# Gate and up of a feed-forward by seven products of quarters (the Winograd form of Strassen's scheme) in a two-block fp32 kernel

## The chip, the cores and the metric

The kernel runs on one core of a Trainium2 chip. The metric is the device time of one execution in microseconds (us); lower is better. All arithmetic is fp32.

## The reference

Two transformer blocks work on x of 256 tokens by 1024. The change concerns the last piece of the second block:

```
h = modulate(rms_norm(x, g_ffn), sh_f, sc_f)
x = x + gt_f * ((silu(h @ w_gate) * (h @ w_up)) @ w_down)
```

w_gate and w_up are 1024 by 2816, w_down is 2816 by 1024. sh_f, sc_f and gt_f are slices of silu(c) @ w_ada + b_ada; only gt_f, the last of them, is made while the feed-forward runs.

## The kernel before, in words

The program is one list of instructions for each engine, written out by hand and tied by semaphores. Every engine works its list in order, so a wait holds everything behind it on that engine.

**Weights.** Weights of 2 MB (a "tile": 8 chunks of 128 rows by 512 columns, or 4 by 1024) stream through a ring of three slots (`wring`, `W_SLOTS`), in the order of `TILES` (`tile_list`, L98), issued by SP at L455. The load of tile n waits until tile n-3 is no longer needed. For the feed-forward the order is gate0, up0, gate1, up1, ada10, gate2, up2, ada11, gate3, ... up5, down0 to down5. gate5, up5 and down5 are half tiles. ada10 and ada11 are two of the twelve parts of w_ada; DVE multiplies each by the row c and sums it, in four chunks of 128x1024 (`ada_sums`, L1553). When ada11 is done, POOL writes the row gt_f out and reads it back to all partitions (`gate_row`, L1433 and L1436); DVE needs it when down is finished.

**Products.** hT2 holds h turned: 8 chunks of 128 features by 256 tokens. Gate and up are made turned too: a 128x128 block of weights is the stationary operand, and chunks of hT2 stream past it. `by_cols` (L543) streams all 256 tokens at once, 8 chunks for each of the 4 column blocks of a tile. `by_block` (L613) streams one block of 128 tokens; gate0 and up0 are made so, since the second block of tokens is turned late (`turn_fed`). An fp32 product stands in the trace as two records of a weight load and two of a matmul.

**Elementwise work.** For each half tile ACT takes the tanh of half the gate sum from PSUM (L1402), DVE multiplies (1 + tanh) by the gate sum (L2178) and that by the up sum (L2181), which gives gT; the factor 0.5 comes in at the end. PSUM banks rotate by `PLAN` and `bank_list`. Down (L1079) takes gT as stationary operand and streams 512 columns of w_down at a time into four sums; DVE scales them by gt_f and adds them to x (L2149, L2150), and SP stores x.

**Just before the feed-forward**, PE makes the last product of w_out (L1041), DVE adds it to x (L2149, L2150), ACT takes the norm, DVE scales (L1495), PE turns the block (L520), and DVE modulates it into hT2 (L1504, L1508).

## Time and profile before

| | |
|---|---|
| median of 3 runs | 1334.63 us (1334.06 to 1335.1) |
| the profiled execution, its own time | 1332.32 us |
| its span, first to last instruction | 1330.5 us |
| PE busy | 1211.0 us (91%) |
| DVE busy | 791.2 us (59%) |
| ACT busy | 231.9 us (17%) |
| moved by DMA | 401 MB, 302 GB/s |
| mean granted clock of PE | 0.973 of 2.4 GHz |

The span is what the trace shows; the profiled execution took 1.8 us more than it, and the median of the runs is 2.3 us above the profiled execution. In the rows below L12 is a line of the kernel before; PE is TensorE's matmuls, PEld its weight loads, which run beside them; DVE, ACT, POOL and SP are the vector, scalar, GpSimd and sync engines. In square brackets or behind the last bar stands the idle time ahead of an instruction and what ended it.

### The profile page before, as it was taken

The numbers are of one execution on the slowest core, as the hardware profiler recorded it, in microseconds if no ns is written. First come the engines' busy times: TensorE is split into PE (matmuls) and PEld (weight loads), VectorE is DVE, ScalarE is ACT, GpSimd is POOL, SyncE is SP. The second block draws the span as 40 slices with busy tenths as digits, with TensorE's granted clock in tenths as the row PEclk, the third lists the DMA queues.
The fourth block names the chain that finished last, engine by engine and source line by source line (L and its number), as shares of the span: only waits on it lengthen the run. The fifth ranks groups of instructions, "written<-read, shape, count | busy, mean of one in ns | idle before, by whom it ended". The sixth has DMA issues, their size and how long they took to land.

```text
span 1330.5 us, 12510 instructions
## 1 busy us (share of the span) xinstructions
PE 1211.0 (91%) x4454; PEld 730.4 (55%) x4454; DVE 791.2 (59%) x1886; ACT 231.9 (17%) x593; POOL 321.6 (24%) x276
## 2 busy tenths in 40 slices
PE   8999999988988887777988887688999899999998
PEld 7657996654554443333333333333466559888743
DVE  4667864589686887686877865655557932220001
ACT  2132210221111111113111112113102511000000
POOL 0100000334544544344445355541000000000000
PEclk9999999999999999799999899989999999999999
DMA  8531658799999999999999999998658534574540
GB/s 312 184 133 64 253 200 321 291 373 406 418 421 420 421 423 415 416 420 410 418 421 422 397 405 422 421 420 339 231 190 252 206 127 156 191 223 143 190 158 32
DMA packets 93789, 401.27 MB, mean 302 GB/s; under 512 B 6496, under 2 KB 9952, under 8 KB 60832
## 3 DMA queue, kind: packets, MB, share of 16 engines
q0 software_dynamic: 37440, 270.30, 49.3%
q1 hardware_dynamic: 56288, 130.18, 27.5%
q8 instruction: 36, 0.59, 0.2%
q14 instruction: 25, 0.20, 0.0%
HBM read 399.39 MB, written 1.06 MB: 301 GB/s over the span
## 4 chain that ended last, share of the span: by engine, by line
PE 60%; DMA 21%; DVE 14%; issue 2%; ACT 2%; POOL 1%; DVEq 0%; SPq 0%
DMA big<-in_peer_uv,idx_t 20%; PE ps L543 18%; PE ps L818 12%; PE ps L531 8%; DVE big L1941 6%; PE ps L1079 6%; PE ps L613 3%; PE ps L691 2%; PE ps L722 2%; PE ps L1041 2%; PE ps L749 2%; PE ps L591 1%; POOL big L1454 1%; DMA wring<-in_w_in 1%; ACT rows L1247 1%
## 5 line engine op out<-in xcount | busy, mean ns | idle before, releaser
L818 PE MATMUL ps<-big,rows 128*128 128x512 f32 x1024 | 482.4, 627 | 107.3 <-ACT rows L1247 107.2
L818 PEld LDWEIGHTS ps<-big,rows 128*128 128x128 f32 x1024 | 199.9, 200 | 371.8 <-issue 371.8
L1454 POOL DMA_INDIRECT big<-in_peer_uv,idx_t x256 | 310.3, 1212 | 377.3 <-PE ps L818 323.0
L1941 DVE CUSTOM_DVE_ANT_0 big<-big 128x1024 f32<-128x1024 f32 x256 | 307.9, 1226 | 139.6 <-DMA big<-in_peer_uv,idx_t 136.7
L543 PE MATMUL ps<-big,wring 128*128 128x256 f32 x1088 | 236.8, 379 | 0.0
L543 PEld LDWEIGHTS ps<-big,wring 128*128 128x128 f32 x1088 | 206.0, 190 | 28.0 <-issue 0.5
L531 PE MATMUL ps<-wring,big 128*128 128x512 f32 (+1 forms) x304 | 126.0, 571 | 0.0
L1241 ACT ACTIVATE small<-small 128x4 f32<-128x4 f32 (+2 forms) x68 | 13.9, 205 | 502.3 <-DVE small L1946 502.3
L531 PEld LDWEIGHTS ps<-wring,big 128*128 128x128 f32 x304 | 57.0, 190 | 62.8 <-issue 61.0
L1247 ACT ACTIVATE rows<-const,small 128x128 f32<-128x128 f32 x256 | 82.2, 390 | 21.1 <-DVE small L1950 21.1
L1079 PE MATMUL ps<-wring,big 128*128 128x512 f32 x176 | 75.7, 592 | 0.0
L2149 DVE SCALAR_TENSOR_TENSOR big<-ps,big 128x512 f32<-128x512 f32 x8 | 5.5, 692 | 91.3 <-PE ps L1079 70.6
L1432 POOL TENSOR_TENSOR small<-small,lane 128x8 f32<-128x8 f32 x2 | 1.2, 624 | 232.2 <-DVE small L1553 232.2
L2181 DVE TENSOR_TENSOR big<-big,ps 128x512 f32<-128x512 f32 x11 | 7.6, 688 | 82.1 <-PE ps L543 74.8
L1079 PEld LDWEIGHTS ps<-wring,big 128*128 128x128 f32 x176 | 33.4, 190 | 41.7 <-issue 41.6
L1553 DVE CUSTOM_DVE_ANT_0 wring<-wring,c_row 128x1024 f32<-128x1024 f32 x40 | 47.2, 1220 | 6.4 <-DMA wring<-in_w_ada 5.0
L749 PEld LDWEIGHTS ps<-big,wring 128*128 128x128 f32 x384 | 46.0, 192 | 9.1 <-issue 9.1
L749 PE MATMUL ps<-big,wring 128*128 128x128 f32 x384 | 46.3, 275 | 0.0
L1127 ACT ACTIVATE big<-ps 128x512 f32<-128x512 f32 (+1 forms) x57 | 31.0, 582 | 73.9 <-PE ps L531 23.8
L613 PE MATMUL ps<-big,wring 128*128 128x128 f32 x320 | 36.3, 275 | 1.0 <-DVE big L1504 1.0
L613 PEld LDWEIGHTS ps<-big,wring 128*128 128x128 f32 x320 | 36.0, 192 | 1.7 <-DVE big L1504 1.2
L1418 POOL DMA_DIRECT2D big<-in_norm_ffn x1 | 0.7, 692 | 137.3 <-DVE big L1736 137.3
(287 smaller groups left out, 988.2 us busy)
## 6 DMA issues: line engine op xcount, KB each, us to landing
wring<-in_w_in SPq DMA_DIRECT2D x16, 2048.0 KB, 8.5
wring<-in_w_ada SPq DMA_DIRECT2D x10, 2048.0 KB, 7.9
wring<-in_w_gate SPq DMA_DIRECT2D x5, 2048.0 KB, 7.7
wring<-in_w_up SPq DMA_DIRECT2D x5, 2048.0 KB, 9.0
wring<-in_w_down SPq DMA_DIRECT2D x5, 2048.0 KB, 7.6
wring<-in_peer_wq SPq DMA_DIRECT2D x4, 2048.0 KB, 20.8
wring<-in_w_out SPq DMA_DIRECT2D x3, 2048.0 KB, 8.4
big<-in_peer_uv,idx_t POOLq DMA_INDIRECT x256, 13.0
```

Source lines behind the costliest of these rows:

```text
L531: last = nc.tensor.matmul(o[:, 0:w], lhs[:, c, b * P:(b + 1) * P], wt[:, c, c0:c0 + w], start=(c == 0), stop=(c == k - 1))
L543: last = nc.tensor.matmul(o[:, c2 * S:(c2 + 1) * S], wt[:, c, n0:n0 + P], src[:, c, :], start=(c == 0), stop=(c == KD - 1))
L613: last = nc.tensor.matmul(o[:, c2 * S + b * P:c2 * S + (b + 1) * P], wt[:, c, n0:n0 + P], src[:, c, b * P:(b + 1) * P], start=(c == 0), st ...
L691: last = nc.tensor.matmul(o[:, c2 * S:(c2 + 1) * S], wt[:, c, n0:n0 + P], lhs[:, c, :], start=(c == 0), stop=(c == 3))
L749: last = nc.tensor.matmul(o[:, n * P:(n + 1) * P], wt[:, c, n * P:(n + 1) * P], h2T[b][:, c, :], start=(c == 0), stop=(c == KD - 1))
L818: last = nc.tensor.matmul(banks[h], diag[:, k % DIAGS, :], v_part[:, ring_at(k), h * 512:(h + 1) * 512], start=False, stop=(k % SLOTS == S ...
L1079: last = nc.tensor.matmul(o, gT[:, f, b * P:(b + 1) * P], wt[:, c, h * 512:(h + 1) * 512], start=(f == 0), stop=(f == FC - 1))
L1127: nc.scalar.activation(dst, bank(name, n) if src is None else src, ACT.Copy).then_inc(emptied(*name), 1)
L1247: nc.scalar.activation(diag[:, k % DIAGS, :], ident, ACT.Copy, scale=w_now[:, at_w:at_w + 1])\
L1454: pool.indirect_dma_start(pair_ring[:, ring_at(k), :], None, a["peer_uv"], bass.IndirectOffsetOnAxis(idx_t[:, k:k + 1], 0))\
L1553: last = nc.vector.tensor_tensor_reduce(w[:, c, :], w[:, c, :], c_row[:, :], 1.0, 0.0, ALU.mult, ALU.add, to[:, c:c + 1])
L1941: nc.vector.tensor_tensor_reduce(u_part[:, ring_at(k), :], u_part[:, ring_at(k), :], h_t[:, b, :], 1.0, 0.0, ALU.mult, ALU.add, a_dot[:, i ...
```

## The change

Each of gate0, gate1, up1, ... gate5, up5 (eleven tiles, numbered j = 0 to 10; up0 stays as eight plain products of each column block and token block) is cut into quarters: two halves f of its columns by two halves k of the 1024 features. hT2 is cut into two halves k by two blocks of tokens b. Seven products of quarters (P1 to P7, `step`) take the place of eight. Each product is 4 chunks for each of 2 column blocks of 128, all with 128 tokens streamed (half tiles: 1 column block).

- DVE makes four sums of weight quarters for each tile (`weight_sums`), each of 4x256 elements a partition, the fourth in place in the ring slot; and four sums of hT2 once (`h_sum`).
- P1, P6, P7 and P4 pile up in one pair of banks, P5 and P3 in another, P2 has its own. After P1, P5, P6, P7 and P4, ACT copies the running sum of 128x256 to SBUF (`part_out`); DVE adds three pairs (`part_added`).
- The gate sum lies in SBUF (ff_g). tanh, its product with (1 + tanh) and the product with up are now one instruction each of 128x1024 for a tile.
- The tiles ada10 and ada11 leave the ring: both go to one buffer of their own, ada10 behind gate1 and ada11 behind gate3. For ada11 SP waits until DVE has summed all of ada10. The ring has up1 right before gate2 and up2 right before gate3. One chunk of 128x1024 of ada10 or ada11 is summed with each of the tiles j = 1 to 8.
- Down has the same products in other banks. It waits for gT tile by tile.

The core of the diff (new buffers, views of them, semaphores and the last loop of DVE, which has the same work as before, are left out):

```diff
@@ -48,7 +48,28 @@
-FF_ADA = {1: 10, 2: 11}
+FF_PRODUCTS = [("gate", 0)] + [(n, i) for i in range(1, 6) for n in ("gate", "up")]
+FF_ADA = {j: (10 + (j - 1) // 4, (j - 1) % 4) for j in range(1, 9)}
+HOME_COUNT = {4: 1, 5: 2, 10: 3, 11: 4}
+FF_ORDER = [("P1", "P2", "P5", "P6", "P3", "P7", "P4")] + [("P1", "P5", "P6", "P3", "P7", "P2", "P4")] * 10
+def pairs_of(i):
+    return min(4, FC - 4 * i) // 2
+def ff_steps(j, product):
+    return 7 * j + FF_ORDER[j].index(product) + 1
+def ff_banks(j):
+    return 2 * (j % 2), 4, 6 + j % 2
@@ -117,8 +138,6 @@
         t += [(f"gate{i}", KD, w, "w_gate", 0, 512 * i), (f"up{i}", KD, w, "w_up", 0, 512 * i)]
-        if i in FF_ADA:
-            t += [ada[FF_ADA[i]]]
     t += [(f"down{i}", min(4, FC - 4 * i), D, "w_down", 512 * i, 0) for i in range(6)]
...
+                    elif before != "up0" and before[:-1] in ("gate", "up"):
+                        sp.wait_ge(step_done, 7 * (FF_PRODUCTS.index((before[:-1], int(before[-1]))) + 1))
...
+                if name in ("gate1", "gate3"):
+                    i = 10 if name == "gate1" else 11
+                    if i == 11:
+                        sp.wait_ge(ada_made, ADA_ORDER.index(10) + 1)
+                    p0 = 512 * ADA_PARTS[i]
+                    sp.dma_start(ada_home2.rearrange("p (c n) -> p c n", c=4),
+                                 a["w_ada"][p0:p0 + 512, :].rearrange("(c p) n -> p c n", p=P)).then_inc(home_landed, 16)
...
@@ -1054,32 +1124,113 @@
-            for h in range(2):
-                reserved("gate0", h)
-            by_block("gate0", 0, hT2)
...
+                sums, w = ff_sums(j), pairs_of(FF_PRODUCTS[j][1])
+                x_bank, z_bank, y_bank = ff_banks(j)
...
+                if product == "P1":
+                    n = TILE_NO["%s%d" % FF_PRODUCTS[j]]
+                    pe.wait_ge(tile_landed[n % W_SLOTS], 16 * (n // W_SLOTS + 1))
+                    if j >= 2:
+                        pe.wait_ge(part_copied, 5 * (j - 1))
+                    else:
+                        bank_free(x_bank)
+                        bank_free(x_bank + 1)
+                    lhs, rhs, o, start = ff_quarter(j, 0, 0), hT2[:, k0, tok[0]], x_bank, True
+                elif product == "P2":
+                    if j >= 2:
+                        pe.wait_ge(part_added, 3 * (j - 1))
+                    else:
+                        bank_free(y_bank)
+                    lhs, rhs, o, start = ff_quarter(j, 0, 1), hT2[:, k1, tok[0]], y_bank, True
+                elif product == "P5":
+                    pe.wait_ge(w_summed, 4 * j + 1)
+                    if j:
+                        pe.wait_ge(part_added, 3 * (j - 1) + 1)
+                    else:
+                        bank_free(z_bank)
+                        bank_free(z_bank + 1)
+                        pe.wait_ge(h_summed, 1)
+                    lhs, rhs, o, start = sums[:, 0], h_sum[:, 0], z_bank, True
+                elif product == "P6":
+                    pe.wait_ge(w_summed, 4 * j + 2)
+                    if j == 0:
+                        pe.wait_ge(h_summed, 2)
+                    pe.wait_ge(part_copied, 5 * j + 1)
+                    lhs, rhs, o, start = sums[:, 1], h_sum[:, 1], x_bank, False
+                elif product == "P3":
+                    pe.wait_ge(w_summed, 4 * j + 3)
+                    pe.wait_ge(part_copied, 5 * j + 2)
+                    lhs, rhs, o, start = sums[:, 2], hT2[:, k1, tok[1]], z_bank, False
+                elif product == "P7":
+                    pe.wait_ge(w_summed, 4 * j + 4)
+                    if j == 0:
+                        pe.wait_ge(h_summed, 3)
+                    pe.wait_ge(part_copied, 5 * j + 3)
+                    lhs, rhs, o, start = ff_quarter(j, 1, 0), h_sum[:, 2], x_bank, False
+                else:
+                    if j == 0:
+                        pe.wait_ge(h_summed, 4)
+                    pe.wait_ge(part_copied, 5 * j + 4)
+                    lhs, rhs, o, start = ff_quarter(j, 1, 1), h_sum[:, 3], x_bank, False
+                for n in range(w):
+                    to = ps[:, o, n * P:(n + 1) * P] if product == "P2" else ps[:, o + n, 0:P]
+                    for c in range(4):
+                        last = nc.tensor.matmul(to, lhs[:, c, n * P:(n + 1) * P], rhs[:, c, :], start=(start and c == 0),
+                                                stop=(c == 3), skip_group_check=True)
+                last.then_inc(step_done, 1)
+            def up_first(b, quarters):
+                wt = tile("up0", KD, 512)
+                for n in quarters:
+                    h, c2 = n // 2, n % 2
+                    o = ps[:, BANK[("up0", h)], :]
+                    for c in range(KD):
+                        last = nc.tensor.matmul(o[:, c2 * S + b * P:c2 * S + (b + 1) * P], wt[:, c, n * P:(n + 1) * P],
+                                                hT2[:, c, b * P:(b + 1) * P], start=(c == 0), stop=(c == KD - 1))
+                    if b == NB - 1 and c2:
+                        begin("up0", h)
+                        last.then_inc(product_done, 1)
+            step(0, "P1")
+            step(0, "P2")
+            reserved("up0", 0)
+            up_first(0, (0,))
             turn_fed(1)
-            for h in range(2):
-                reserved("up0", h)
-            by_block("up0", 0, hT2)
-            wait_turned("n5T", [1])
-            by_block("gate0", 1, hT2)
-            by_block("up0", 1, hT2)
-            for i in range(1, 6):
-                by_cols(f"gate{i}", TILES[TILE_NO[f"gate{i}"]][2], hT2)
-                by_cols(f"up{i}", TILES[TILE_NO[f"up{i}"]][2], hT2)
-            outs = [begin("down", b, h) for b in range(NB) for h in range(2)]
+            up_first(0, (1,))
+            reserved("up0", 1)
+            up_first(0, (2, 3))
+            for product in ("P5", "P6", "P3", "P7"):
+                step(0, product)
+            up_first(1, (0, 1))
+            step(0, "P4")
+            up_first(1, (2, 3))
+            for j in range(1, len(FF_PRODUCTS)):
+                for product in FF_ORDER[j]:
+                    step(j, product)
             for i in range(6):
-                pe.wait_ge(ff_ready, min(2 * i + 2, FC // 2))
-                for n, o in enumerate(outs):
+                pe.wait_ge(ff_ready, i + 1)
+                if i == 0:
+                    pe.wait_ge(part_copied, 5 * (end - 2))
+                    pe.wait_ge(part_added, 3 * (end - 1))
...
@@ -1393,14 +1544,32 @@
                 act.wait_ge(x_whole, 5 + b)
                 rms(4, b)
             exp_and_tanh()
-            for i in range(6):
-                for h in range(2 if i < 5 else 1):
-                    n = 2 * i + h
-                    wait_product(act, f"gate{i}", h)
-                    if n >= 1:
-                        act.wait_ge(ff_ready, n)
-                    nc.scalar.activation(ff_e, bank((f"gate{i}", h)), ACT.Tanh, scale=0.5).then_inc(ff_exp, 1)
+            def part_out(j, product, n, to):
+                act.wait_ge(step_done, ff_steps(j, product))
+                nc.scalar.activation(to, sums_in(j, n), ACT.Copy).then_inc(part_copied, 1)
+            def gate_tanh(j):
+                i = FF_PRODUCTS[j][1]
+                act.wait_ge(part_added, 3 * j + 3)
+                act.wait_ge(part_copied, 5 * j + 5)
+                w = 512 * pairs_of(i)
+                nc.scalar.activation(ff_e[:, 0:w], ff_g[:, 0:w], ACT.Tanh, scale=0.5).then_inc(ff_exp, 1)
+            for j, (kind, i) in enumerate(FF_PRODUCTS):
+                if j >= 2:
+                    act.wait_ge(part_added, 3 * (j - 1))
+                part_out(j, "P1", 0, part_at(j, 0))
+                part_out(j, "P5", 1, part_at(j, 1))
+                if j >= 2 and kind == "up":
+                    gate_tanh(j - 1)
+                part_out(j, "P6", 0, part_at(j, 2))
+                part_out(j, "P7", 0, part_at(j, 3))
+                if kind == "gate" and i:
+                    act.wait_ge(ff_ready, i)
+                part_out(j, "P4", 0, ff_out(j, 1, 0))
+                if j == 0:
+                    gate_tanh(0)
...
@@ -2161,37 +2330,108 @@
+            def weight_sums(j, which):
+                sums, q = ff_sums(j), [[ff_quarter(j, f, k) for k in range(2)] for f in range(2)]
+                n = TILE_NO["%s%d" % FF_PRODUCTS[j]]
+                if which[0] == 0:
+                    dve.wait_ge(tile_landed[n % W_SLOTS], 16 * (n // W_SLOTS + 1))
+                    if j >= 2:
+                        dve.wait_ge(step_done, 7 * (j - 1))
+                for m in which:
+                    if m == 0:
+                        tt(sums[:, 0], q[1][0], q[1][1], ALU.add).then_inc(w_summed, 1)
+                    elif m == 1:
+                        dve.wait_ge(w_summed, 4 * j + 1)
+                        tt(sums[:, 1], sums[:, 0], q[0][0], ALU.subtract).then_inc(w_summed, 1)
+                    elif m == 2:
+                        dve.wait_ge(w_summed, 4 * j + 2)
+                        tt(sums[:, 2], q[0][1], sums[:, 1], ALU.subtract).then_inc(w_summed, 1)
+                    else:
+                        tt(q[1][0], q[0][0], q[1][0], ALU.subtract).then_inc(w_summed, 1)
             mixed_added(0, 0)
             mixed_added(1, 0)
             scale(4, 0)
             mixed_added(0, 1)
             dve.wait_ge(modc_ready, 2)
             turned("n5T", 0, hT2, modc[:, 3 * KD:4 * KD], modc[:, 2 * KD:3 * KD])
+            weight_sums(0, (0, 1, 2))
             mixed_added(1, 1)
+            weight_sums(0, (3,))
             scale(4, 1)
             turned("n5T", 1, hT2, modc[:, 3 * KD:4 * KD], modc[:, 2 * KD:3 * KD])
-            for i in range(6):
-                for h in range(2 if i < 5 else 1):
-                    n = 2 * i + h
-                    dve.wait_ge(ff_exp, n + 1)
-                    link(stt(ff_e, ff_e, 1.0, bank((f"gate{i}", h)), ALU.add, ALU.mult))
-                    dve.sem_inc(emptied(f"gate{i}", h), 1)
-                    wait_product(dve, f"up{i}", h)
-                    tt(gT[:, 2 * n:2 * n + 2, :].rearrange("p c t -> p (c t)"), ff_e, bank((f"up{i}", h)), ALU.mult)\
-                        .then_inc(ff_ready, 1)
-                    dve.wait_ge(ff_ready, n + 1)
-                    dve.sem_inc(emptied(f"up{i}", h), 1)
-                if i in FF_ADA:
-                    ada_sums(FF_ADA[i], range(4))
+            for h in range(2):
+                wait_moved(dve, "n5T", 1, h)
...
+            tt(h_sum[:, 0], fed[0][1], fed[0][0], ALU.subtract).then_inc(h_summed, 1)
+            dve.wait_ge(h_summed, 1)
+            tt(h_sum[:, 1], fed[1][1], h_sum[:, 0], ALU.subtract).then_inc(h_summed, 1)
+            tt(h_sum[:, 2], fed[1][1], fed[0][1], ALU.subtract).then_inc(h_summed, 1)
+            dve.wait_ge(h_summed, 2)
+            tt(h_sum[:, 3], fed[1][0], h_sum[:, 1], ALU.subtract).then_inc(h_summed, 1)
+            def gated(j):
+                dve.wait_ge(ff_exp, i + 1)
+                stt(ff_g[:, 0:w], ff_e[:, 0:w], 1.0, ff_g[:, 0:w], ALU.add, ALU.mult).then_inc(ff_gated, 1)
+            def fed_out(j):
+                dve.wait_ge(part_copied, 5 * j + 5)
+                dve.wait_ge(part_added, 3 * j + 3)
+                dve.wait_ge(ff_gated, i + 1)
+                to = gT[:, 4 * i:4 * i + 2 * pairs_of(i), :].rearrange("p c t -> p (c t)")
+                tt(to, to, ff_g[:, 0:w], ALU.mult).then_inc(ff_ready, 1)
+            for j, (kind, i) in enumerate(FF_PRODUCTS):
+                ahead = j + 1 < len(FF_PRODUCTS)
+                if ahead:
+                    weight_sums(j + 1, (0, 1))
+                if j == 1:
+                    gated(0)
+                    dve.wait_ge(ff_gated, 1)
+                    for h in range(2):
...
+                        last = tt(gT[:, 2 * h:2 * h + 2, :].rearrange("p c t -> p (c t)"), ff_g[:, h * 512:(h + 1) * 512],
+                                  bank(("up0", h)), ALU.mult)
+                        last.then_inc(emptied("up0", h), 1)
...
+                    dve.sem_inc(ff_ready, 1)
+                elif kind == "up":
+                    gated(j - 1)
+                elif j > 1:
+                    fed_out(j - 1)
+                if kind == "gate" and i:
+                    dve.wait_ge(ff_ready, i)
+                dve.wait_ge(step_done, ff_steps(j, "P3"))
+                dve.wait_ge(part_copied, 5 * j + 3)
+                tt(ff_out(j, 0, 1), part_at(j, 2), sums_in(j, 1), ALU.add).then_inc(part_added, 1)
+                if ahead:
+                    weight_sums(j + 1, (2, 3))
+                if j in FF_ADA:
+                    n, c = FF_ADA[j]
+                    ada_sums(n, [c])
+                dve.wait_ge(part_copied, 5 * j + 4)
+                tt(ff_out(j, 1, 1), part_at(j, 3), part_at(j, 1), ALU.add).then_inc(part_added, 1)
+                dve.wait_ge(step_done, ff_steps(j, "P2"))
+                tt(ff_out(j, 0, 0), part_at(j, 0), sums_in(j, 2), ALU.add).then_inc(part_added, 1)
+            fed_out(len(FF_PRODUCTS) - 1)
...
```

## Rows read from the trace of the kernel before

**Rows 1.** The page: span, PE busy, granted clock in 40 slices.
```profile
span 1330.5 us, 12510 instructions
...
PE 1211.0 (91%) x4454; PEld 730.4 (55%) x4454; DVE 791.2 (59%) x1886; ACT 231.9 (17%) x593; POOL 321.6 (24%) x276
...
PEclk9999999999999999799999899989999999999999
```

**Rows 2.** Chain that ended last: start us, us, what, records.
```profile
1097.31 7.14 PE ps L613 x64
...
1105.33 21.44 PE ps L613 x192
1126.77 124.32 PE ps L543 x576
1251.09 75.55 PE ps L1079 x176
```

**Rows 3.** Stretches: us, busy by engine (records), PEclk, DMA share, GB/s.
```profile
1105.33:1126.77 21.44, 21.44 (x193) 21.44 (x193) 4.35 (x7) 1.19 (x2) 0.00 (x0) 1.00 0.28 99
1126.77:1251.09 124.32, 124.32 (x577) 109.44 (x577) 21.73 (x34) 5.37 (x9) 1.73 (x3) 1.00 0.56 190
324.00:330.00 6.00, 3.99 (x7) 1.69 (x7) 5.53 (x17) 1.96 (x6) 1.27 (x2) 0.79 1.01 416
330.00:336.00 6.00, 6.00 (x23) 3.29 (x22) 5.39 (x24) 1.63 (x6) 3.08 (x4) 0.93 1.04 409
```

**Rows 4.** Timeline of PE among the experts: start us, us, what, records.
```profile
326.12 8.80 PE L818 MATMUL ps<-big,rows 128*128 128x512 f32 x16 [2.01 <-ACT rows L1247]
...
335.65 1.95 PE L749 MATMUL ps<-big,wring 128*128 128x128 f32 x16
337.44 7.03 PE L818 MATMUL ps<-big,rows 128*128 128x512 f32 x16
```

**Rows 5.** Groups by line and shape, DVE: busy us, mean ns, idle.
```profile
L1553 DVE CUSTOM_DVE_ANT_0 wring<-wring,c_row 128x1024 f32<-128x1024 f32 x40 | 47.2, 1220 | 6.4 <-DMA wring<-in_w_ada 5.0 <-DVE big L2041 0.7 <-DVE big L2181 0.4
...
L2181 DVE TENSOR_TENSOR big<-big,ps 128x512 f32<-128x512 f32 x11 | 7.6, 688 | 82.1 <-PE ps L543 74.8 <-PE ps L613 7.3
...
L1666 DVE TENSOR_TENSOR big<-big 128x1024 f32<-128x1024 f32 x4 | 4.9, 1219 | 0.0
...
L2125 DVE TENSOR_TENSOR big<-ps,small 128x256 f32<-128x256 f32 x4 | 1.7, 425 | 0.1
```

**Rows 6.** The same view, ACT.
```profile
L1152 ACT ACTIVATE big<-big 128x1024 f32<-128x1024 f32 x2 | 2.1, 1057 | 6.5 <-DVE big L1565 6.5
...
L1127 ACT ACTIVATE big<-ps 128x256 f32<-128x256 f32 x4 | 1.6, 389 | 11.1 <-PE ps L782 10.2 <-PE ps L790 0.9
```

**Rows 7.** Waits, 1128 to 1250 us: total us, times, longest us.
```profile
DVE big L2181 <- PE ps L543: 69.2, 8, 12.5
```

**Rows 8.** DMA issues, 947.7 to 948.5 us: count, KB, us to landing.
```profile
wring<-in_w_in SPq DMA_DIRECT2D x1, 2048.0 KB, 8.4
big<-in_w_ada SPq DMA_DIRECT2D x1, 2048.0 KB, 13.1
```

**Rows 9.** DMA issues, 200 to 215 us.
```profile
wring<-in_w_out SPq DMA_DIRECT2D x1, 2048.0 KB, 10.0
big<-in_w_out SPq DMA_DIRECT2D x1, 2048.0 KB, 14.9
```

**Rows 10.** Timeline of POOL at the last modulation row.
```profile
1188.19 0.97 POOL L1433 DMA_DIRECT2D gate_out<-small  x1 [0.30 <-POOL small L1432]
```

**Rows 11.** DMA issue of gate4 at 1187.64 us.
```profile
wring<-in_w_gate SPq DMA_DIRECT2D x1, 2048.0 KB, 12.3
```

**Rows 12.** Timeline ahead of the feed-forward, DVE.
```profile
1092.99 0.69 DVE L1508 TENSOR_TENSOR big<-big,small 128x512 f32<-128x512 f32 x1
...
1097.35 0.69 DVE L2149 SCALAR_TENSOR_TENSOR big<-ps,big 128x512 f32<-128x512 f32 x1 [3.67 <-PE ps L1041]
...
1100.61 0.75 DVE L1495 TENSOR_SCALAR big<-x_t,rstd 128x1024 f32<-128x1024 f32 x1 [1.84 <-ACT rstd L1123]
```

More of the change, by code:

```diff
@@ L176, in product_list @@
     p += [("out2_0", 0), ("catT", 1), ("out2_1", 0), ("out2_0", 1)] + half("n5T", 0)
-    p += [("out2_1", 1)] + half("n5T", 1) + cols("gate0") + cols("up0")
-    for i in range(1, 6):
-        for n in (f"gate{i}", f"up{i}"):
-            p += cols(n, 2 if i < 5 else 1)
-    p += [("down", b, h) for b in range(NB) for h in range(2)]
+    p += [("out2_1", 1)] + half("n5T", 1) + cols("up0")
     return p
 PLAN = {name: n for n, name in enumerate(product_list())}
+LAST_BANKS = {("out2_0", 1): 6, ("n5T", 0, 0): 2, ("n5T", 0, 1): 3, ("out2_1", 1): 7, ("n5T", 1, 0): 4, ("n5T", 1, 1): 5,
+              ("up0", 0): 2, ("up0", 1): 3}
 def bank_list():
@@ L197, in bank_list @@
             bank[name] = 4
+        elif name in LAST_BANKS:
+            bank[name] = LAST_BANKS[name]
         elif name == ("n3T", 1, 0):
@@ L327, in two_blocks @@
         gT = at(big, 2048, FC * S).rearrange("p (c t) -> p c t", c=FC)
-        ff_e = at(big, 7680, 512)
+        ff_sum = [at(big, 8192 + 3072 * i, 3072) for i in range(2)]
+        h_sum = at(big, 14336, 2048).rearrange("p (n c t) -> p n c t", n=4, c=4)
+        parts = [at(big, 16384 + 1024 * i, 1024) for i in range(2)]
+        ff_g, ff_e = at(big, 18432, 1024), at(big, 19456, 1024)
+        ada_home2 = at(big, 22528, TILE)
         tmp2 = at(big, 28416, 1024)
@@ L1070, in _, with bank_free, step @@
-            outs = [begin("down", b, h) for b in range(NB) for h in range(2)]
+            def bank_free(n):
+                pe.wait_ge(bank_emptied[n], sum(v == n for v in BANK.values()))
+            def step(j, product):
+                sums, w = ff_sums(j), pairs_of(FF_PRODUCTS[j][1])
+                x_bank, z_bank, y_bank = ff_banks(j)
+                k, tok = (slice(4 * n, 4 * n + 4) for n in range(2)), [slice(b * P, (b + 1) * P) for b in range(NB)]
+                k0, k1 = k
+                if product == "P1":
[49 more added lines that the diff above has]
+                last.then_inc(step_done, 1)
@@ L1071, in _ @@
+            end = len(FF_PRODUCTS)
             for i in range(6):
-                k = TILES[TILE_NO[f"down{i}"]][1]
+                k = 2 * pairs_of(i)
                 wt = tile(f"down{i}", k, D)
-                pe.wait_ge(ff_ready, min(2 * i + 2, FC // 2))
-                for n, o in enumerate(outs):
+                pe.wait_ge(ff_ready, i + 1)
+                if i == 0:
+                    pe.wait_ge(part_copied, 5 * (end - 2))
+                    pe.wait_ge(part_added, 3 * (end - 1))
+                for n, o in enumerate(DOWN_BANKS):
@@ L2187, in _ @@
-            dve.wait_ge(mod_ready, 32)
-            for b in range(NB):
-                for h in range(2):
-                    wait_product(dve, "down", b, h)
-                    if b == 1:
-                        dve.wait_ge(x_ready, h + 1)
-                    gated_add(bank(("down", b, h)), mod[:, 1, :], b, slice(h * 512, (h + 1) * 512),
-                              tmp2[:, h * 512:(h + 1) * 512], 0.5).then_inc(x_ready, 1)
+            for h in range(2):
+                wait_moved(dve, "n5T", 1, h)
@@ new lines, in _ @@
+            fed = [[hT2[:, 4 * k:4 * k + 4, b * P:(b + 1) * P] for b in range(NB)] for k in range(2)]
+            tt(h_sum[:, 0], fed[0][1], fed[0][0], ALU.subtract).then_inc(h_summed, 1)
[4 more added lines that the diff above has]
+            tt(h_sum[:, 3], fed[1][0], h_sum[:, 1], ALU.subtract).then_inc(h_summed, 1)
@@ new lines, in _ @@
+            fed_out(len(FF_PRODUCTS) - 1)
+            dve.wait_ge(mod_ready, 32)
+            for n in range(2 * NB):
+                b, h = n // 2, n % 2
+                c = slice(h * 512, (h + 1) * 512)
+                t = tmp2[:, h * 512:(h + 1) * 512]
+                dve.wait_ge(last_done, n + 1)
+                if b == 1:
+                    dve.wait_ge(x_ready, h + 1)
+                link(stt(t, ps[:, DOWN_BANKS[n], :], 0.5, mod[:, 1, c], ALU.mult, ALU.mult))
+                tt(x[:, b, c], x[:, b, c], t, ALU.add).then_inc(x_ready, 1)
```

50 lines of the change are left out of this document (42 added, 8 removed).

## Prediction

> **What bounds the kernel now.** I read the page first, then the chain of waits, then the stretches. The page has PE busy for 91% of the span at nearly full clock [rows 1]. The chain from the end of the last w_out product on is PE alone: 7.14 + 21.44 us of 128-token pieces, 124.32 us of 256-token pieces, 75.55 us of down [rows 2]. In both gate and up stretches PE is busy for the whole time at a granted clock of 1.00 (the 2.4 GHz level), with DVE busy for a fifth or less [rows 3]. Others wait for PE there and PE for nobody: DVE alone 69.2 us in 8 waits [rows 7]. So here time is PE time, as long as what the change gives DVE, ACT and the loads stays beside it.
>
> **PE's work.** The pieces of 128 tokens (L613) are 64 + 192 records in 28.58 us, 111.6 ns each, so one product (two records) takes 223.3 ns. Those of 256 tokens (L543) are 576 records in 124.32 us, 215.8 ns each, 431.7 ns a product [rows 2]. Together 152.9 us. After the change all pieces have 128 tokens: gate0 56, up0 64, eight full tiles 8 x 56 = 448, two half tiles 2 x 28 = 56, in sum 624 products x 223.3 ns = 139.3 us. PE gains 13.6 us: an eighth of the work goes (17.9 us), the narrower pieces give 4.3 us back, since the weight loads fill the whole of such a stretch (PEld 21.44 of 21.44 us against 109.44 of 124.32 us [rows 3]).
>
> Does the rate hold with much going on beside it? Among the experts 16 records of the same shape take from 335.65 to 337.44, 111.9 ns each [rows 4], with DMA at 409 GB/s and DVE busy for 90% [rows 3]. I take 111.6.
>
> **DVE and ACT.** One full tile takes PE 56 x 0.2233 = 12.50 us, a product of quarters (8 pieces) 1.79 us. DVE's sum of two 128x1024 operands costs 1.22 us, 512 wide 0.69, 256 wide 0.43 (from PSUM; I take it for the SBUF pair too), a chunk of w_ada 1.22 [rows 5]. For each full tile DVE has four sums (4.9), one gating product (1.2), three additions (1.3), one chunk (1.2): 8.6 us of 12.5. ACT has five copies at 0.39 and every second tile a tanh of 1.06 [rows 6]: 2.5 us on average. A copy lies beside the next product, which uses other banks: 0.39 + about 0.1 of signals against 1.79. The closest chain in steady state: DVE's third addition of a gate tile, tanh, the copy of P6, P7. P7 starts 7.15 us into the up tile, so the tanh may start as late as 7.15 - 0.05 - 0.39 - 1.06 = 5.6 us into it; the addition is done 0.8 us ahead of the tile. All this I cost at nothing; the cover is the 3.9 us that DVE has free in each tile.
>
> **The start.** DVE's three sums for gate0 stand between the modulation of the first token block, done at 1092.99 + 0.69, and the last w_out addition, which began at 1097.35 [rows 12]: 3.66 us in a hole of 3.67. Allow 0.15 us. The fourth sum lies in the 1.84 us in which DVE waits for the norm [rows 12]. PE comes to the second turning after 24 pieces, at 1097.31 + 5.36 = 1102.67; the scaling is done by about 1101.5. The sums of hT2 (4 x 0.69) are started by 1106 and the first is ready at about 1106.7; P5 of gate0 needs it at 1108.9. Cost nothing. up1 can only be loaded when gate0's P4 is through, 24.1 us after 1097.31, and takes 8.4 us as a lone load [rows 8]. DVE stands at it until 32.6, and its P3 addition of gate1 comes at about 38; P5 of up1 needs that at 42.0. Cost nothing, with 4 us to spare.
>
> **The ring at up3.** Here I expect a stall. SP may issue ada11 only when DVE has summed the last chunk of ada10, in the tile up2, and up3 stands behind ada11 in SP's list. Count from the end of up2 on PE. P3 of up2 ends at -5.35; DVE then adds (0.43), makes two sums (2.44) and the chunk (1.22), and with signals SP issues ada11 at about -0.9, up3 0.4 later. Two loads issued together landed 8.4 and 13.1 us after issue [rows 8], elsewhere 10.0 and 14.9 [rows 9]: the second about 5 us behind the first. So up3 lands at about 12.6. DVE's very next item at 0 is the sums of up3, so it stands for 12.6 us with gate3's additions behind it. Then two sums (2.44), the gating of up2 (1.22) and gate3's first addition (0.43) with signals: 16.9. That addition frees the bank pair that P5 of up3 wants. PE ends gate3 at 12.5, waits about 0.2 for up3 itself, makes P1 until 14.5 and stands until 16.9: **2.4 us**. The rest of DVE's list (two sums, chunk, two additions) ends at 21.5, then tanh and the P6 copy end at 23.0, where P7 could have begun at 22.3: **0.7 us**. Together about 3.4 us. gate4, issued behind up3, lands 5 us after it, at 17.7, and DVE wants it at 21.4: nothing more.
> Bounds: no stall at all, if ada11 goes out early or up3 overtakes it; or up3 a full lone load (8.4 us) after ada11 in place of 5, 3.3 us more, so 6.7 us. I take 3.4, from the pairs of loads.
>
> **The rest.** Down begins when up5 ends; down0 is issued as up4 ends, 12.5 us before it is wanted. Beside the write of gt_f [rows 10] a load took 12.3 us [rows 11], and the same write now falls there: 0 to 0.5 us, I take 0. Down (75.55 us) and the last additions stay. Waits already met cost PE nothing in the alternation of rows 4. ACT copies and takes exp among the experts with no table load between them, so the copies bring none.
>
> **The sum.** -13.6 + 3.4 = -10.2 us; signals and the start 0.1. The profiled execution, 1332.3 us (span 1330.5 [rows 1]), would take 1322.2. The median of the runs is 2.3 us above it: 1324.5 us.
>
> **The rivals.**
> *No stall at up3*: the whole 13.6 us, 1321.0 us. For it: the loads leave the DMA half idle (share 0.56 [rows 3]). Against it: the order of SP's and DVE's lists.
> *A longer stall at up3*: the bound of 6.7 us, and perhaps the clock. In the stretch from 324 us, with a wait of 2.01 us, the clock stood at 0.79 [rows 3] and 16 wide records took 8.80 us against 7.03 [rows 4]: 1.8 us more. That is 1334.6 - 13.6 + 6.7 + 1.8 = 1329.5 us.
> *PE shows its waits*: 77 products start behind waits that PE did not have. At 0.1 us each, 7.7 us more: 1332 us, no change. Against it stand rows 4, where such waits cost nothing. From 0.13 us each there is no gain left.
> *DVE becomes the bound, and the kernel slower*: the place is the sums and gating products, five a tile. At a price s DVE's tile is 5s + 3 us with signals, against 12.5: it binds from s = 1.9. Before that the stall at up3 grows with s, so at 1.9 the gain is used up. If the four-chunk views, one of them written into the ring slot beside PE's reads, doubled the price to 2.44, the tile would be 15.2 us: 8 x 2.7 = 21.6 us, and a longer stall at the start and at up3 of about 7, less the 13.6 gained and some overlap, gives about 1350 us. Against it: 1.22 us in every row of that size, chunks written in a ring slot included [rows 5].
> *Narrow pieces cost more than half of wide ones*: the change makes 992 more records of 128 tokens. At 0.6 of a wide record in place of 0.52 (129.5 ns for 111.6) they take 17.8 us more, 1342 us. Against it: the rate of rows 2 and 4. The Trainium skill (TensorE: Matmul & The Clock Gate, Back-to-back issue gap) gives 81 ns for 128 columns and 131 ns for 512 in a stream of bf16 loads and matmuls; an estimate on a straight line between them is 98 ns for 256, so that half the width costs 0.83 of the whole, which here would be 67 us over the forecast, about 1391 us. The trace disagrees for fp32: 111.6 against 215.8 ns, 0.52.
>
> **How the numbers follow.** Forecast with a stall of 2 to 5 us: 0.63. No stall: 0.08. Longer stall: 0.15. Waits shown: 0.07. DVE bound: 0.06. Narrow pieces: 0.01. The range 1320.5 to 1330.5 takes the first three. A measurement of this kernel can tell 0.2%, 2.7 us. Faster: the first three and a fourth of the waits' case, 0.88; same 0.05; slower 0.07.
>
> **What would show it.** Some 1248 records of 128 tokens at 111.6 ns, no 256-token records in gate and up. DVE's sums at 1.22 us, ACT's copies at 0.39. One DMA wait of DVE of about 12 us for the tile of w_up, behind it one PE wait of some 2.4 us ended by a DVE addition and one under 1 us ended by an ACT copy; up3 landing near 13 us after issue. Down starting about 10 us earlier. The forecast is wrong if PE idles ahead of most products, if the sums take over 1.5 us, or if a second tile's load is waited for on PE.

## The result, and the profile after

The changed kernel takes 1345.0 us (median of 4 runs, 1344.52 to 1347.55) where the kernel before takes 1334.82: a ratio of 1.0083, 95% interval 1.007 to 1.0095 (all ratios here are worked out from the single runs, not from the two medians, which give 1.0076). It is slower by 10 us; the forecast was 10 us faster, 1324.5 us in a range of 1320.5 to 1330.5. All ratios are of fast runs: one run of the kernel before, of the 13 beside e5 to e8, took 4420 us in the slow state and is left out of them. The span of its profiled execution is 1342.7 us, 12.2 more than before [rows 1]. In what follows the changed kernel's lines are: L1184 the matmuls of the seven products, L1195 those of up0, L1230 down, L1111 w_out, L590 the turning of the norm; on DVE L2343, L2346, L2349 and L2351 are the four sums of a tile, L2379 and L2389 the gating products, L2400 the products with up0, L2414 the addition that frees the banks of P5 and P3, L2421 and L2423 the other two, L1722 a chunk of w_ada; L1550 on ACT copies a partial sum.

The chain of waits of the changed kernel, from the last w_out product on (start us, us, what; compare [rows 2]):

```profile
1093.99 6.87 PE ps L1111 x16
1100.86 3.57 PE ps L1184 x32
...
1123.17 1.80 PE ps L1184 x16
1124.97 0.02 issue
1124.99 7.72 DMA wring<-in_w_up
...
1136.39 1.30 DVE big L2400 x2
1137.68 0.14 issue
1137.82 46.98 PE ps L1184 x400
...
1189.09 13.11 DMA wring<-in_w_up
...
1205.88 0.43 DVE big L2414
1206.31 0.14 issue
1206.44 37.61 PE ps L1184 x320
1244.06 0.02 issue
1244.07 17.21 DMA wring<-in_w_down
1261.29 0.04 issue
1261.33 77.51 PE ps L1230 x176
```

Before, this chain was PE alone. Now it runs three times through a load. The same three places in the timeline of PE (in square brackets PE's idle time and what ended it), with one ahead of them:

```profile
1086.01 7.11 PE L1111 MATMUL ps<-wring,big 128*128 128x512 f32 x16 [1.60 <-DVE x_t L2319]
...
1137.82 3.75 PE L1184 MATMUL ps<-big,wring 128*128 128x128 f32 x16 [9.29 <-DVE big L2400]
...
1206.44 7.22 PE L1184 MATMUL ps<-big 128*128 128x128 f32 x48 [2.01 <-DVE big L2414]
...
1220.65 5.52 PE L1184 MATMUL ps<-big 128*128 128x128 f32 x48
...
1261.33 0.99 PE L1230 MATMUL ps<-wring,big 128*128 128x512 f32 x1 [4.78 <-DMA wring<-in_w_down]
```

Stretches of the changed kernel, in the columns of rows 3:

```profile
1137.80:1141.40 3.60, 3.58 (x17) 3.60 (x18) 0.00 (x0) 0.00 (x0) 0.00 (x0) 0.50 0.00 0
...
1141.40:1204.27 62.87, 62.87 (x561) 62.84 (x560) 30.95 (x39) 11.11 (x26) 0.00 (x0) 0.99 0.43 154
1204.27:1213.50 9.23, 7.22 (x50) 7.09 (x49) 9.16 (x12) 2.49 (x5) 0.00 (x0) 0.82 0.88 327
```

**Where the 12.2 us came from.** Gate and up, from the end of w_out to the start of down, took 1097.31 to 1251.09 before, 153.8 us, and 1100.86 to 1261.33 now, 160.5 us. The matmuls are what was counted: the stretch from 1141.40 has 561 records in 62.87 us, 112 ns each, and 139.3 us + 0.9 us of turning make 140.2. The other 20.3 us are waits and the clock behind them: 9.3 us at gate1 and 1.8 us since its first 16 records take 3.54 us (1137.82 to 1141.36) and not 1.79; 2.0 us at up3 and 1.7 us in the 48 records behind it (7.22 us against 5.52 in a later tile); 4.8 us at down0; 0.7 us in smaller parts. Down takes 77.5 us in place of 75.6, again with a lowered clock. The 3.5 us by which the stage starts later are 1.6 us of the wait at 1086, 0.6 us of clock (the first and the third of the four w_out products take 7.21 and 7.11 us, not 6.87), and 1.4 us by which the first w_out product started later, at 1069.89 against 1068.53 us. These 1.4 us say nothing of the change: in two executions of one and the same kernel further down (e4 and e12) that start is at 1070.98 and at 1068.87. In sum 6.7 + 2.0 + 3.5 = 12.2.

### The profile page after: what moved, and what is told of

Read it like the earlier page. It is cut to its first block, busy times and chain, and to the rows that moved or that the text cites. A ratio compares the mean times of both kernels' runs of the same rounds, so it can differ in the third digit from the quotient of the medians.

```text
span 1342.7 us, 13525 instructions
## 1 busy us (share of the span) xinstructions
PE 1206.8 (90%) x4870; PEld 737.7 (55%) x4870; DVE 849.9 (63%) x1958; ACT 250.8 (19%) x643; POOL 319.9 (24%) x276
## 4 chain that ended last, share of the span: by engine, by line
PE 53%; DMA 25%; DVE 17%; issue 2%; ACT 2%; POOL 1%; SPq 0%; DVEq 0%; ACTq 0%
DMA big<-in_peer_uv,idx_t 20%; PE ps L888 9%; PE ps L613 8%; PE ps L601 8%; PE ps L1184 7%; DVE big L2110 7%; PE ps L1230 6%; PE ps L1111 2%; PE ps L761 2%; PE ps L792 2%; PE ps L819 2%; DMA wring<-in_w_up 2%; DMA wring<-in_w_in 1%; DMA wring<-in_w_down 1%; PE ps L661 1%
## 5 line engine op out<-in xcount | busy, mean ns | idle before, releaser
L613 PE MATMUL ps<-big,wring 128*128 128x256 f32 x512 | 112.3, 379 | 0.0
L613 PEld LDWEIGHTS ps<-big,wring 128*128 128x128 f32 x512 | 96.6, 190 | 13.2 <-issue 0.5
L1184 PE MATMUL ps<-big,wring 128*128 128x128 f32 x640 | 75.6, 279 | 9.3 <-DVE big L2400 9.3
L1230 PE MATMUL ps<-wring,big 128*128 128x512 f32 x176 | 77.5, 603 | 4.8 <-DMA wring<-in_w_down 4.8
L1184 PEld LDWEIGHTS ps<-big,wring 128*128 128x128 f32 x640 | 74.3, 195 | 9.9 <-DVE big L2400 9.4
L1230 PEld LDWEIGHTS ps<-wring,big 128*128 128x128 f32 x176 | 33.9, 193 | 47.7 <-issue 42.7
L1184 PE MATMUL ps<-big 128*128 128x128 f32 x480 | 57.5, 281 | 2.0 <-DVE big L2414 2.0
L1184 PEld LDWEIGHTS ps<-big 128*128 128x128 f32 x480 | 56.6, 198 | 2.2 <-issue 2.2
L2433 DVE SCALAR_TENSOR_TENSOR big<-ps,big 128x512 f32<-128x512 f32 x4 | 2.8, 691 | 77.0 <-PE ps L1230 77.0
L819 PEld LDWEIGHTS ps<-big,wring 128*128 128x128 f32 x384 | 46.0, 192 | 9.1 <-issue 9.1
L819 PE MATMUL ps<-big,wring 128*128 128x128 f32 x384 | 46.3, 275 | 0.0
L1550 ACT ACTIVATE big<-ps 128x256 f32<-128x256 f32 (+1 forms) x55 | 19.9, 365 | 125.6 <-PE ps L1184 119.1
```

Of the source, the lines that this page charges most:

```text
L613: last = nc.tensor.matmul(o[:, c2 * S:(c2 + 1) * S], wt[:, c, n0:n0 + P], src[:, c, :], start=(c == 0), stop=(c == KD - 1))
L819: last = nc.tensor.matmul(o[:, n * P:(n + 1) * P], wt[:, c, n * P:(n + 1) * P], h2T[b][:, c, :], start=(c == 0), stop=(c == KD - 1))
L1184: last = nc.tensor.matmul(to, lhs[:, c, n * P:(n + 1) * P], rhs[:, c, :], start=(start and c == 0), stop=(c == 3), skip_group_check=True)
L1230: last = nc.tensor.matmul(ps[:, o, :], gT[:, f, b * P:(b + 1) * P], wt[:, c, h * 512:(h + 1) * 512], start=(f == 0), stop=(f == FC - 1))
```

## The experiments

The kernels e1 to e4 were run together, then e5 to e8, then e9 to e12. Each batch had the kernel before beside it, with medians of 1333.86, 1334.86 and 1334.59 us. Ratios are to that, with 95% intervals. The changed kernel itself was not run in these batches, so a difference to its 1345.0 us is good to about 1 us; the traces, between two marks of the same execution, tell more.

**The wait at gate1.** In DVE's loop, gate0's gating and the products with up0 ahead of the sums of up1:

```diff
-                if ahead:
+                if ahead and j != 1:
                     weight_sums(j + 1, (0, 1))
                 if j == 1:
...
                     dve.sem_inc(ff_ready, 1)
+                    weight_sums(2, (0, 1))
```

> The changed kernel with one reordering in DVE's list: at gate1 the gating of gate0 and its product with up0 stand ahead of the weight sums of up1, not behind them. Theory (the first product of gate1 wants the banks that up0 was summed in, and DVE empties them only after it has waited for the load of up1): PE's wait of 9.3 us at the start of gate1 falls to about 1.5 us, the 1.8 us of lowered clock behind it go too, 9 to 10 us less than the changed kernel: about 1335.5 us. Rival (PE stands there for the load of up1 itself or for the sums made from it): the wait stays near 9 us and the time near 1345 us.

Measured: 1336.19 us, 1.0019 (1.0006 to 1.0031), against 1345.0 for the changed kernel. The timeline of PE:

```profile
1130.66 2.02 PE L1184 MATMUL ps<-big,wring 128*128 128x128 f32 x16 [0.87 <-DVE big L2400]
```

That is 8.8 us less, 9 to 10 were expected. The wait fell from 9.29 to 0.87 us and the 16 records from 3.75 to 2.02. The load of up1 takes as long as it did; PE did not need it. P1 of gate1 writes banks 2 and 3 (`ff_banks(1)`), and the change gives these to up0 too (`LAST_BANKS`). DVE's products with up0 empty them, and stood behind the sums of up1, which wait for its load. Here DVE still waits for up1's load until 1134.26 us, 3.6 us after PE has begun gate1; so the rival, that PE needs the load itself or the sums made from it, is out.

**The wait at down0.** POOL's last step:

```diff
             pool.wait_ge(ada_made, ADA_ORDER.index(11) + 1)
+            pool.wait_ge(down_used, 2)
             gate_row(1)
```

> The changed kernel with POOL's write and reading back of the last modulation row held until two tiles of down are used up; DVE needs the row only at the end. Theory (the 4 KB write in pieces of 4 bytes, issued 1.9 us ahead of down0, slows down0's load from about 8 to 17.2 us): down0 lands 8 to 9 us after issue, PE's 4.8 us wait for it goes and the 2 us of lowered clock in down as well, 1338 to 1340 us. Rival (the loads of down are slow at this place by themselves): down0 still takes over 14 us and the time stays near 1345 us.

Measured: 1338.52 us, 1.0038 (1.0027 to 1.005). 6 to 7 us less than the changed kernel's, as expected. PE has no wait at down0, and the stage reads, in its chain:

```profile
1207.36 50.10 PE ps L1184 x432
1257.46 75.55 PE ps L1230 x176
```

Down is back at 75.55 us. The landing of down0, first here, then in the changed kernel (DMA issues at 1244.98 and 1244.07 us):

```profile
wring<-in_w_down SPq DMA_DIRECT2D x1, 2048.0 KB, 9.2
```

```profile
wring<-in_w_down SPq DMA_DIRECT2D x1, 2048.0 KB, 17.2
```

POOL's write in the changed kernel:

```profile
1242.18 0.97 POOL L1602 DMA_DIRECT2D gate_out<-small  x1 [0.30 <-POOL small L1601]
```

It is issued 1.9 us ahead of down0, and its signal lets POOL go on at 1252.43 us. From 1244.07 to 1252.40 us the DMA engines move 35 GB/s at a busy share of 0.46; from there to 1261.30 us 330 GB/s at 0.89. With the row late, 1244.00 to 1252.40 us has 252 GB/s. So the load hardly moved until the write was done, and then took about what a lone load takes.

To see which half of POOL's step does it, only the reading back was held:

```diff
                 pool.wait_ge(gates_out, 16 * (j + 1))
+                if j == 1:
+                    pool.wait_ge(down_used, 2)
                 pool.dma_start(mod[:, j, :], gate_out[j].partition_broadcast(P)).then_inc(mod_ready, 16)
```

> The changed kernel in which POOL writes the last modulation row out at once, as there, but reads it back to all partitions only after two tiles of down. Theory (the write in pieces of 4 bytes alone slows down0's load): down0 still lands 15 to 18 us after issue, PE still waits 4 to 5 us for it, time near 1345 us. Rival (the reading back of 512 KB is what down0 shares the queues with): down0 lands in 9 to 13 us, no wait, 1338 to 1340 us.

Measured: 1345.95 us, 1.0078 (1.0057 to 1.0099); down0 landed after 16.0 us, PE waited 3.6 us for it. So the write of 4 KB alone makes most of the delay: 16.0 us against the 8.0 to 9.3 us of the seven traces in which the write comes later (e2, e4, e8 to e12). The four traces of kernels with both halves of the step there have 17.2, 17.4, 17.7 and 18.3 us, so reading back seems to add 1 to 2 us; that rests on a single trace of e6.

**The stall at up3, the one that was forecast.** ada11 moved behind up3 in SP's list:

```diff
-                if name in ("gate1", "gate3"):
+                if name in ("gate1", "up3"):
```

> The changed kernel with the load of ada11 moved in SP's list from behind gate3 to behind up3, so that up3 waits for nothing but its slot. Theory of the prediction (up3 lands late because it stands behind a wait for DVE's last sum of ada10 and then behind ada11 in the queue, DVE stands for it, and PE stands for DVE's addition that frees its banks): DVE's 12.9 us wait goes, PE's 2.0 us wait with it and the 1.7 us of lowered clock behind it, about 1341 us. Rival (the stall at up3 is made up later, since DVE has slack): about 1345 us, with PE's time spent at another wait.

Measured: 1343.77 us, 1.0078 (1.0057 to 1.0099), 1.2 us less where 4 were expected. The wait at up3 is gone, the rest of the gain was given back at the next place:

```profile
1138.90 3.61 PE L1184 MATMUL ps<-big,wring 128*128 128x128 f32 x16 [9.31 <-DVE big L2400]
1259.17 16.08 PE L1230 MATMUL ps<-wring,big 128*128 128x512 f32 x30 [5.88 <-DMA wring<-in_w_down]
```

down0 landed 18.3 us after issue here, not 17.2, so the wait at down0 grew by 1.1 us, and down took 78.76 us, 1.25 more (its chain). Whether the edit made the load later is not shown: with the same write beside it e5 has 17.4 and e1 17.7 us. Measured between the same two instants (end of w_out, end of down) the kernel gained 2.0 us, 236.0 against 238.0.

**The wait ahead of the feed-forward.** `LAST_BANKS` gives the second block of the first w_out half bank 6, which still holds the first block of the other half:

```diff
-LAST_BANKS = {("out2_0", 1): 6, ("n5T", 0, 0): 2, ...
+LAST_BANKS = {("out2_0", 1): 0, ("n5T", 0, 0): 2, ...
```

> The changed kernel with the second block of the first w_out half in bank 0 in place of bank 6, nothing else. Theory (ahead of the feed-forward PE waits 1.6 us for DVE to empty bank 6): PE's wait of 1.60 us before the third of the four w_out products goes, and up to 0.5 us of clock behind it: 1343 us, 1.6 to 2 us less than the changed kernel. Rival (that time is lost again at the next wait, since DVE is as late as before): 1345 us and PE waits elsewhere ahead of the first product of gate0.

Measured: 1344.24 us, 1.0076 (1.0055 to 1.0097). The wait of 1.60 us is not in the timeline and no other took its place; the time is 0.8 us lower, which the runs (1342.4 to 1346.3) don't tell from none. The traces do: from the start of the first w_out product to the start of gate0 they have 28.8 us here (1069.13 to 1097.91), as before, and 31.0 us in the changed kernel, 2.2 us for the wait and the clock behind it.

**All four.**

> All of it together: up0 products ahead of up1's sums, the last modulation row late, ada11 behind up3, and the second block of the first w_out half summed in bank 0 in place of bank 6, whose reader DVE was waited for (1.6 us). Theory (the seven products save 13.6 us, and four waits with the clock behind them gave back more than that): 1345.0 less 9.6, 6.8, 3.9 and 2.0, about 1322.5 us, faster than before by some 12 us. Rival (128-wide pieces or the many waits of PE cost by themselves): no less than 1330 us though the four waits are gone.

Measured: 1322.17 us, 0.9921 (0.9896 to 0.9945), and in a second batch:

> The version without the four waits once more, beside the one with the split wait on the same chip: 1322 us, 0.99 of the kernel before.

1322.42 us, 0.9915 (0.9897 to 0.9932). That is 12 us faster than the kernel before. The chain from the end of w_out in the first of them:

```profile
1123.86 3.59 PE ps L1195 x32
1127.45 0.02 issue
1127.47 0.70 DVE big L2401
1128.17 0.14 issue
1128.30 112.80 PE ps L1184 x1008
1241.10 75.55 PE ps L1230 x176
```

1008 records in 112.80 us are 111.9 ns each, with seven products a tile behind waits, against 111.6 in the forecast. PE still waits 0.87 us at gate1 and nowhere else in the stage. Gate and up take 1099.76 to 1241.10, 141.3 us, 12.4 less than before. The rival that many waits cost PE by themselves is out.

**The stall at up3 by itself.** The same with ada11 ahead of up3 again:

> The version without the four waits, but with ada11 behind gate3 again, ahead of up3, as the changed kernel has it: the stall that the prediction counted, alone. Theory (two sizes: PE waits 2 to 2.4 us for DVE's addition, and 1.7 us of lowered clock follow, which the prediction left to its upper bound): 3.5 to 4 us more than the version without, about 1326 us; up3 lands near 13.1 us after issue. Rival (the clock falls only when it had fallen at gate1 before): PE's wait is 2 us and the time about 1324.5 us.

Measured: 1325.55 us, 0.9934 (0.9918 to 0.9951), 3.1 us above the version without it in the same batch (1322.42). Its waits and its timeline:

```profile
DVE big L2344 <- DMA wring<-in_w_up: 17.0, 2, 13.2
...
PE ps L1184 <- DVE big L2416: 2.2, 1, 2.2
```

```profile
1194.53 7.22 PE L1184 MATMUL ps<-big 128*128 128x128 f32 x48 [2.15 <-DVE big L2416]
```

From the end of w_out to down it takes 1099.12 to 1244.63, 145.5 us, 4.2 more: 2.15 of wait, 1.7 of clock, 0.3 in small parts. This is the forecast's mechanism at nearly its size, in a kernel where only the 0.87 us at gate1 stand beside it.

**The price of narrow pieces.** The kernel before, gate1 to up5 in pieces of 128 tokens:

```diff
+                        for b in range(NB if narrow else 1):
                             for c in range(KD):
+                                    t = slice(b * P, (b + 1) * P)
+                                    last = nc.tensor.matmul(o[:, c2 * S + b * P:c2 * S + (b + 1) * P], wt[:, c, n0:n0 + P],
+                                                            src[:, c, t], start=(c == 0), stop=(c == KD - 1))
```

> The kernel before with gate1 to up5 made in pieces of 128 tokens as gate0 is, eight products of quarters, no sums, the same waits, loads and elementwise work. Theory (two pieces of 128 tokens at 223.3 ns take the place of one at 431.7): 288 x 14.9 ns = 4.3 us more than the kernel before, 1338 to 1339 us. Rival (PE hides it or 128-wide pieces cost more over a long stretch): under 2 us or over 6 us more.

Measured: 1338.78 us, 1.0031 (1.002 to 1.0042), 3.9 us more. In the chain:

```profile
1130.79 128.64 PE ps L547 x1152
1259.42 75.55 PE ps L1086 x176
```

128.64 against 124.32 us [rows 2], 4.3 us, 111.7 ns a record.

**How much room DVE has.** In the version without the four waits, additions into a spare buffer ahead of the first and of the third sum of each tile, two at each place (e8) or three (e10):

```diff
                 for m in which:
+                    if j and m in (0, 2):
+                        for _ in range(2):
+                            spare = h_t[:, 0, 0:512 * pairs_of(FF_PRODUCTS[j][1])].rearrange("p (c w) -> p c w", c=4)
+                            link(tt(spare, q[0][0], q[0][1], ALU.add))
```

> The version without the four waits, with four more DVE additions of 128x1024 for every tile from gate1 on (512 wide for the half tiles), into a spare buffer. They add work and leave the output as it is. Theory (DVE has 12.5 - 8.6 = 3.9 us to spare in each tile and 4 x 1.24 = 5.0 us are added): DVE becomes the bound at about 13.9 us a tile with signals, 8 x 1.4 = 11 us more than the version without: about 1333 us, PE waiting once or twice in each full tile. Rival (DVE's additions are not near the bound, or its waits overlap more than the sum says): less than 4 us more.

Measured: 1322.85 us, 0.9912 (0.9892 to 0.9933): no more than without (0.7 and 0.4 us above the two medians of that version). The theory, with 11 us more, failed; the rival, under 4 us, holds. Its timeline of DVE, two starts of a tile's additions:

```profile
1142.88 2.47 DVE L2346 TENSOR_TENSOR big<-wring 128x1024 f32<-128x1024 f32 x2
1145.39 1.22 DVE L2348 TENSOR_TENSOR big<-wring 128x1024 f32<-128x1024 f32 x1
1146.65 1.22 DVE L2351 TENSOR_TENSOR big<-big,wring 128x1024 f32<-128x1024 f32 x1
1147.79 1.22 DVE L2384 SCALAR_TENSOR_TENSOR big<-big 128x1024 f32<-128x1024 f32 x1
1148.93 0.41 DVE L2420 TENSOR_TENSOR big<-big,ps 128x256 f32<-128x256 f32 x1
...
1155.86 2.48 DVE L2346 TENSOR_TENSOR big<-wring 128x1024 f32<-128x1024 f32 x2
```

A tile takes DVE 12.98 us, not 13.9. Operations shown as 1.22 us start 1.14 us apart where nothing is awaited between them, those of 256 elements 0.33 apart. DVE is then 0.5 us a tile slower than PE, and its lead swallows that for eight tiles: PE waits 1.1 us in all beside the 0.87 at gate1. With two additions more:

> The version without the four waits, with six more DVE additions of 128x1024 for each tile from gate1 on. They add work and leave the output as it is. Theory (with four more a tile took DVE 13.0 us, since a row of 1.22 us holds DVE for 1.14; two more make 15.5 us against PE's 12.5, and DVE's lead of some 5 us is then used up in two tiles): 8 x 3.0 - 5 = some 19 us more than the version without, about 1341 us, PE waiting in nearly every full tile. Rival (DVE is not what PE would wait for next): less than 6 us more.

Measured: 1340.94 us, 1.0059 (1.004 to 1.0078), 18.5 us above the version without in the same batch; 19 were expected. DVE is the bound there (120 of 122 us busy in the stretch from 1128 us), and the waits of PE show in which forms that comes:

```profile
PE ps L1184 <- ACT big L1550: 7.8, 4, 2.3
PE ps L1184 <- DVE big L2420: 5.8, 4, 1.6
PE ps L1184 <- DVE big L2354: 3.7, 4, 1.0
```

The 7.8 us are copies that stand behind a tanh, which waits for DVE's last addition: the chain that the prediction called the closest.

**The last wait.** In the version without the four waits P1 of gate1 still waited 0.87 us.

```diff
                         bank_free(x_bank)
-                        bank_free(x_bank + 1)
+                        if j == 0:
+                            bank_free(x_bank + 1)
...
                 for n in range(w):
+                    if (j, product, n) == (1, "P1", 1):
+                        bank_free(x_bank + 1)
```

> The version without the four waits, and the first product of gate1 waits for the second of up0's banks only ahead of its second column block, which is the one that writes it. Theory (PE's last wait in gate and up, 0.87 us for DVE's second product with up0, lies beside the 0.89 us of the first column block): no wait of PE over 0.2 us is left in gate and up and 0.9 to 1.1 us go, about 1321.2 us. Rival (the first column block waits for DVE as well): no difference.

Measured: 1322.11 us, 0.9912 (0.9895 to 0.9928). No wait of PE is left in gate and up, and they take 1099.90 to 1240.49, 140.6 us, 0.75 less. In the time of the runs (1319.7 to 1324.9) it does not show against 1322.42.

## Why the prediction was wrong, point by point

- **PE's work** was right: 624 products at 223.3 ns, the narrow pieces' 4.3 us (4.3 measured alone), 0.3 us of loss at the seams of all products (e4). The 13.6 us are there: without the four waits 12.4 of them show in the stage, 13.2 without the fifth. The rival of narrow pieces reads the page as one on bf16; the section that it cites gives its 81 and 131 ns without a number type.
- **"The start. ... Cost nothing, with 4 us to spare"** is the step that failed most: 11.1 us. It saw DVE standing at up1's load, here from about 1121 to 1132.7 (32.6 us after the stage's start by its count, 31.9 measured), but asked only when P5 of up1 would want gate1's addition. It did not ask who waits for the other thing behind that load in DVE's list, the products with up0, and took banks of the first two tiles for free. The code has them: `bank_free(x_bank)` for j = 1, with up0 in the same banks. The prediction's own times give the wait, as an estimate: behind 32.6 us DVE has two sums (2.4), a gating product (1.2) and the two products with up0 (1.4), done at 37.6; PE is through with up0 at 24.1 + 3.6 = 27.7; so PE stands for 9.9 us. Measured were 9.29 us, and 1.8 us of clock. e1 showed the cause: 9.29 us to 0.87.
- **The same step left out the hole ahead of it**: moving `("out2_0", 1)` to bank 6 made PE wait 1.60 us for DVE. The sum had no term for `LAST_BANKS`. e5 took the wait away; in the total it is within the spread.
- **"0 to 0.5 us, I take 0"** at down0 cost 4.8 us and 2 us of clock. The row taken for it [rows 11] was gate4's load, issued at 1187.64, 0.5 us ahead of POOL's write [rows 10]. down0 is issued 1.9 us behind the write and lands after 17.2 us. e2 and e6 put it on the write. The row was near in kind and not in order.
- **The stall at up3** was right in place and cause: up3 landed 13.1 us after issue (forecast about 13), DVE's wait was 12.9 (12.6), PE's 1.96 to 2.15 (2.4). The 0.7 us at P7 did not come. PE's lowered clock is not needed for that: e1 kept its speed behind the stall and had no wait at P7 either. In it the prediction's costs were too high:

```profile
1197.28 5.60 PE L1184 MATMUL ps<-big 128*128 128x128 f32 x48 [2.06 <-DVE big L2415]
1202.73 7.38 PE L1184 MATMUL ps<-big,wring 128*128 128x128 f32 x64
```

  From the addition that PE waits for to the end of DVE's last one there are 4.1 us in e1 (1197.13 to 1201.22), not 4.6, and tanh and copy are done 1.4 us later, not 1.5, at 1202.58, as PE comes to P7. What did come and was not in the sum are 1.7 us of lowered clock, which stood among the rivals. e9 has 3.1 us in the runs, 4.2 in the stretch, against 3.4 forecast. That these are near is in part luck: the waits came out 1.2 us shorter than the sum had them, and 1.7 us of clock came on top.
- **DVE and ACT** were rightly costed at nothing once the tiles run evenly. The room was under-stated: 1.14 us hold DVE where 1.22 was taken (e8). The slower rival, DVE as the bound, was not what made the kernel slower; e10 shows that it would be, at 15.5 us a tile.
- **The chances** had 0.07 for slower, 0.06 on DVE's price and 0.01 on that of narrow pieces. None of the cases was a bank shared between the plain products of up0 and the new ones.

## What to carry to other kernels

For every load that an engine starts to wait for in its list, go through all that stands behind it up to the next item with room, and for each ask who waits for it, banks included. A new bank plan is read entry by entry against the last reader of each bank. A load's time is taken from a row with the same neighbour on the same side: a load issued behind a write in tiny pieces is another case than one ahead of it. A saving on the bounding engine is worth its full size only when every such wait is gone: here one and the same saving of 13.6 us read as 10 us lost, or 12 gained, by four edits of a line or two.

## What the runs showed of the hardware

- A write of 4 KB in pieces of 4 bytes (so its access pattern), issued 1.9 us ahead, takes a 2 MB load from 9.2 to 17.2 us; POOL waited 9.3 us for the write's signal, and until then 35 GB/s were moved. The Trainium skill (DMA: Bandwidth & Descriptors, Why small descriptors are slow) has a fixed cost for each packet and each descriptor. The trace fits that, with 9.3 us for 4 KB; how much of it is either cost, no run here shows.
- A wait costs PE more than its length when the granted clock falls. After 9.29 us the first 16 records are at a granted clock of 0.50, the 1.2 GHz level, and take twice their time; after 1.96 to 2.15 us 48 records took 7.22 us for 5.52, in five of the six traces with the stall at up3 (5.60, with 2.06 us, in e1). With six more sums, waits of 2.35 us left the clock at 1.00:

```profile
1175.09 7.38 PE L1184 MATMUL ps<-big,wring 128*128 128x128 f32 x64 [2.35 <-ACT big L1550]
1174.00:1183.00 9.00, 7.91 (x71) 7.94 (x72) 8.83 (x9) 2.10 (x5) 0.00 (x0) 1.00 0.01 2
```

  So the length of a wait alone does not tell whether the clock falls; what else decides it stays open.
- Operations of DVE of 128x1024 that are shown as 1.22 us start 1.14 us apart where no wait lies between them, and 1.26 apart where one does (e8). A sum of shown durations overstates a busy DVE: 12.98 us a tile where such a sum, with signals, gave 13.9.
